# A hybrid RWKV-7 / block-attention layer on one core: ScalarE's weight split moved to the head of each RWKV chunk, and two attention score tiles moved ahead of the last chunk's root and transposed output

## The reference, cut to what matters

```
h   = RMSNorm(x);  P = h @ W_in          # columns: RWKV parts | q k v of attention | gate_A | gate_B
y_A = RWKV-7 time mixing, 8 heads of 64  # per head a 64x64 state, delta rule, then GroupNorm, bonus, gate
      per head:  y = (y - mean) * rsqrt(var + eps) * ln_w + ln_b   (+ bonus, * g)
y_B = causal block attention with ALiBi, 8 heads of 64 (softmax over scores)
x   = x + (sigmoid(gate_A) * (y_A @ W_up_A) + sigmoid(gate_B) * (y_B @ W_up_B)) @ W_o
x   = x + SwiGLU(RMSNorm(x));  out = RMSNorm(x)
```

## Time and profile before

| | |
|---|---|
| median of three runs | 932.14 us (931.51 to 936.15) |
| the profiled execution | 935.92 us, of which the span from first to last instruction is 934.1 us |
| mean granted TensorE clock over the span | 0.953 of full |
| busy: TensorE matmul, weight load | 887.8 us, 701.1 us |
| busy: VectorE, ScalarE, GpSimd | 413.5, 331.4, 120.7 us |
| RWKV chunks | from about 148 to 322 us |
| attention tiles | from about 322 to 464 us |

### The profile page before, as it was taken

How to read it: one execution, slowest core, us unless ns; L and a number is a source line. 1 busy time by engine, 2 the same in 40 slices (tenths; PEclk the granted TensorE clock), 3 DMA queues, 4 the chain that set the end, 5 groups by cost and what they waited for, 6 DMA issues and landing times.

```text
span 934.1 us, 12038 instructions
## 1 busy us (share of the span) xinstructions
PE 887.8 (95%) x4561; PEld 701.1 (75%) x4561; DVE 413.5 (44%) x600; ACT 331.4 (35%) x509; POOL 120.7 (13%) x124
## 2 busy tenths in 40 slices
PE   5999998999999969999999989999999999999996
PEld 4677766868686847666788867888888888888884
DVE  5389596241414144444466246443444344322224
ACT  5667422121212143333444145344443344211222
POOL 3054921130304011101032000000000000000000
PEclk9999999696968789999999999999999999999998
DMA  6422423210113112222233513333333332232212
GB/s 188 114 70 67 135 69 90 53 48 16 34 34 102 57 45 68 69 68 57 65 105 118 170 50 95 108 90 90 90 97 105 98 104 90 94 105 94 91 68 90
DMA packets 122298, 79.45 MB, mean 85 GB/s; under 512 B 15033, under 2 KB 110322, under 8 KB 122258
## 3 DMA queue, kind: packets, MB, share of 16 engines
q1 hardware_dynamic: 122066, 78.87, 28.5%
q0 software_dynamic: 192, 0.02, 0.0%
HBM read 73.63 MB, written 5.24 MB: 84 GB/s over the span
## 4 chain that ended last, share of the span: by engine, by line
PE 84%; DVE 8%; ACT 4%; issue 2%; DMA 1%; POOL 0%; SPq 0%; ACTq 0%; DVEq 0%
PE PS L1469 24%; PE PS L1470 23%; PE PS L1471 23%; DVE w_lo L1097 2%; PE PS L1670 2%; PE PS L1688 1%; PE PS L1565 1%; PE PS L1821 1%; DVE sq L1171 1%; PE PS L1832 1%; ACT w_hi L763 1%; PE PS L1636 1%; DVE gates L1376 1%; PE PS L1710 1%; PE PS L1607 1%
## 5 line engine op out<-in xcount | busy, mean ns | idle before, releaser
L1469 PE MATMUL PS<-hT_hi,w_hi 128*128 128x512 f32 (+1 forms) x664 | 275.4, 415 | 9.5 <-DVE gates L1376 5.5
L1470 PE MATMUL PS<-hT_lo,w_hi 128*128 128x512 f32 (+1 forms) x664 | 264.5, 398 | 0.0
L1471 PE MATMUL PS<-hT_hi,w_lo 128*128 128x512 f32 (+1 forms) x664 | 263.9, 397 | 0.0
L1097 DVE TENSOR_TENSOR w_lo<-wraw,w_hi 128x1024 fp32r<-128x1024 f32 (+1 forms) x125 | 165.4, 1324 | 181.2 <-ACT w_hi L763 179.5
L763 ACT ACTIVATE w_hi<-wraw 128x1024 fp32r<-128x1024 f32 (+1 forms) x125 | 131.4, 1051 | 135.3 <-PE PS L1471 112.6
L1469 PEld LDWEIGHTS PS<-hT_hi,w_hi 128*128 128x128 f32 (+1 forms) x664 | 127.0, 191 | 46.1 <-issue 18.6
L1471 PEld LDWEIGHTS PS<-hT_hi,w_lo 128*128 128x128 f32 (+1 forms) x664 | 127.4, 192 | 28.8
L1470 PEld LDWEIGHTS PS<-hT_lo,w_hi 128*128 128x128 f32 (+1 forms) x664 | 127.6, 192 | 24.8 <-issue 1.0
L1470 PE MATMUL PS<-w_lo,act_hi 128*128 128x512 f32 x176 | 70.2, 399 | 0.0
L1469 PE MATMUL PS<-w_hi,act_hi 128*128 128x512 f32 x176 | 69.3, 394 | 0.0
L1471 PE MATMUL PS<-w_hi,act_lo 128*128 128x512 f32 x176 | 69.0, 392 | 0.0
(11 more groups left out here) (234 smaller groups left out, 1092.3 us busy)
## 6 DMA issues: line engine op xcount, KB each, us to landing
wraw<-in_w_ffn_in_dram SPq DMA_DIRECT2D x88, 256.0 KB, 3.1
wraw<-in_w_in_dram SPq DMA_DIRECT2D x82, 256.0 KB, 3.3
wraw<-in_w_ffn_out_dram SPq DMA_DIRECT2D x44, 256.0 KB, 2.9
wraw<-in_w_o_dram SPq DMA_DIRECT2D x16, 256.0 KB, 3.1
xt<-in_x_dram SPq DMA_DIRECT2D x4, 512.0 KB, 5.2
qk_scratch<-stage SPq DMA_DIRECT2D x8, 256.0 KB, 2.7
qkT<-qk_scratch SPq DMA_DIRECT2D x4, 512.0 KB, 4.8
wraw<-in_w_up_a_dram SPq DMA_DIRECT2D x8, 256.0 KB, 3.1
```

Source lines behind the costliest of these rows:

```text
L1097: dve.tensor_tensor(w_lo[:, q, 0:n], wraw[:, s, 0:n], w_hi[:, q, 0:n].bitcast(F32), ALU.subtract)\
L1469: pe.matmul(out_, a_hi, b_hi, start=start, stop=False)
L1470: pe.matmul(out_, a_hi, b_lo, start=False, stop=False)
L1471: return pe.matmul(out_, a_lo, b_hi, start=False, stop=stop)
```

## The change

It touches the order of instructions, and adds one small one. In each chunk, ScalarE's `split_hi` of unit U_QK+2c+3 goes from behind `y_affine(c-1)` to the head of the chunk, ahead of `tokens(c)`. At the seam:

- ScalarE: a one-element Exp ACTIVATE is added ahead of `split_hi(29)`; `ystd(3)` goes behind `probs(0)`; `y_affine(3)` goes behind `probs(1)` and `probs_T(0)`; `ya_hi(3)` goes from tile 0 to tile 1.
- VectorE: `split_lo(29)` goes ahead of `y_centre(3)`; `score_bias(0)` goes ahead of `y_var(3)`; then `weights(0)`, `score_bias(1)`, `y_rstd(3)`, the gate copy of tile 0, `weights(1)`, `split_lo(30)`; `ya_lo(3)` goes to tile 1.
- TensorE: `gate(0, 1)` goes ahead of `probs_T(0)`, then `y_T(3)`; `values(0)` goes behind `gate(1, 0)` and `attn_scores(2)`.

```diff
@@ -974,11 +974,11 @@
                                scale=1.0 if n % 2 else -HD ** -0.5).then_inc(fill_ready, 1)
 
             for c in range(TT):
+                split_hi(U_QK + 2 * c + LEAD, U_QK + 2 * c + LEAD)
                 tokens(c)
                 fill_out(2 * c)
                 if c:
                     y_affine(c - 1)
-                split_hi(U_QK + 2 * c + LEAD, U_QK + 2 * c + LEAD)
                 join_32(c, 0)
                 join_32(c, 1)
                 join_64(c, 0)
@@ -989,8 +989,10 @@
                 if c + 1 < TT:
                     split_hi(U_QK + 2 * c + 1 + LEAD, U_QK + 2 * c + 1 + LEAD)
                 fill_out(2 * c + 1)
-                ystd(c)
-
+                if c + 1 < TT:
+                    ystd(c)
+
+            act.activation(warm[:, 1:2], warm[:, 0:1], ACT.Exp)
             split_hi(U_GATE + LEAD - 1, U_GATE + LEAD - 1)
 
             def probs(m):
@@ -1017,13 +1019,15 @@
                 act.activation(obT_hi[:, p, :], PS[:, 1, :], ACT.Copy).then_inc(obhi_ready, 1)
 
             probs(0)
-            y_affine(TT - 1)
+            ystd(TT - 1)
             for m in range(TT * NP_):
                 if m + 1 < TT * NP_:
                     probs(m + 1)
                 probs_T(m)
+                if m == 0:
+                    y_affine(TT - 1)
                 split_hi(U_GATE + m + LEAD, U_GATE + m + LEAD)
-                if m == 0:
+                if m == 1:
                     ya_hi(TT - 1)
                 if m % TT == TT - 1:
                     ob_hi(m // TT)
@@ -1331,10 +1335,12 @@
                 if more:
                     split_lo(U_QK + 2 * c + 1 + LEAD, U_QK + 2 * c + 1 + LEAD)
                     state(c)
+                else:
+                    split_lo(U_GATE + LEAD - 1, U_GATE + LEAD - 1)
                 y_centre(c)
-                y_var(c)
-                y_rstd(c)
-            split_lo(U_GATE + LEAD - 1, U_GATE + LEAD - 1)
+                if more:
+                    y_var(c)
+                    y_rstd(c)
 
 
             dve.memset(ss[:, 0, 0:1], 0.0).then_inc(gmul_ready, 2)
@@ -1365,17 +1371,25 @@
                 dve.tensor_tensor(obT_lo[:, p, :], PS[:, 1, :], obT_hi[:, p, :].bitcast(F32), ALU.subtract)\
                    .then_inc(oblo_ready, 1)
 
+            def gate_copy(m):
+                dve.wait_ge(w_used, U_GATE + m + 1)
+                dve.tensor_copy(gates[:, KD - 1 - m // 2, m % 2, :], PS[:, 0, :]).then_inc(gates_stored, 1)
+
             score_bias(0)
+            y_var(TT - 1)
             weights(0)
-            for m in range(TT * NP_):
+            score_bias(1)
+            y_rstd(TT - 1)
+            gate_copy(0)
+            weights(1)
+            split_lo(U_GATE + LEAD, U_GATE + LEAD)
+            for m in range(1, TT * NP_):
                 if m + 1 < TT * NP_:
                     score_bias(m + 1)
-                if m + 1 < TT * NP_:
                     weights(m + 1)
-                dve.wait_ge(w_used, U_GATE + m + 1)
-                dve.tensor_copy(gates[:, KD - 1 - m // 2, m % 2, :], PS[:, 0, :]).then_inc(gates_stored, 1)
+                gate_copy(m)
                 split_lo(U_GATE + m + LEAD, U_GATE + m + LEAD)
-                if m == 0:
+                if m == 1:
                     ya_lo(TT - 1)
                 if m % TT == TT - 1:
                     ob_lo(m // TT)
@@ -1868,11 +1882,16 @@
                 gate(m, 0)
                 if m + 1 < TT * NP_:
                     attn_scores(m + 1)
-                probs_T(m)
-                gate(m, 1)
                 if m == 0:
+                    gate(0, 1)
+                    probs_T(0)
                     y_T(TT - 1)
-                values(m)
+                else:
+                    if m == 1:
+                        values(0)
+                    probs_T(m)
+                    gate(m, 1)
+                    values(m)
 
 
             pe.wait_ge(yalo_ready, TT)
```

## The result

The changed kernel takes 886.69 us, median of four runs (885.59 to 888.3), against 931.83 us for the kernel before: the ratio is 0.9554, with a 95% interval of 0.9503 to 0.9605. The forecast was 916 us with a range of 909 to 922.5. The sign was right; the gain was 45 us where 16 were forecast.

What follows compares the result with a forecast made beforehand. TensorE was taken as the bound, its matmuls filling 95% of the span, so only its waits and low-clock stretches could give time. 4.9 us from the chunks plus 11.4 from the seam, 16.3, off 932.14 gave 916 us, range 909 to 922.5.

Steps and rivals of the forecast that it cites:

- What the clock does with part 1 is the open term: Chunks: moving the split leaves the low-clock stretches unchanged, taken as 0, bounds 3.4 us saved or lost.
- the sign of this failure: Listed under what would show the prediction wrong: more than 9 us, or less than 3, from the chunks.
- the clock gains as well: Chunks: without the 1.53 us wait the clock falls later, 1.7 us for each of four chunks; 909 us, chance 0.08.
- Part 1, the waits: Chunk head: the earlier split removes TensorE's waits at `merge_32` for VectorE's negated copy, 4.9 us over four chunks.
- The 0.9 us kept for a late load: Chunk 0: at twice the median load time, `tokens(0)` is 0.9 us late; taken as 0, kept for the range.
- Part 2, the seam: Seam: TensorE's waits of 4.0, 2.9 and 1.8 us and the low clock behind them go; 11.4 us, bounds 6 and 11.7.
- the forecast cover: Seam: GpSimd scales until 328.6, TensorE wants the result at 329.4 for `y_T(3)`, so 0.8 us to spare.
- the seam keeps half its waits: Seam: root, reciprocal and scaling come late, so TensorE stands at `y_T(3)` instead; 921.5 us, chance 0.12.
- nothing: Chunks: `minus_32` is bound by something else, so the chunk part does nothing it says; 920.7 us, chance 0.03.
- nothing measurable: Chunks and seam: new waits take the place of each old one; 932 us, chance 0.03.
- The slower one: Chunks: the clock's return fails once behind `solve`, 22.1 us of work takes 22.1 us more; 938 us, chance 0.03.

Runs made afterwards that it cites:

- late_c0: The changed kernel with ScalarE's split in its old place in chunk 0 alone; five runs at 885.40, 886.87, 887.41, 888.34 and 896.77 us.

## Why the prediction was right or wrong

**The failed step** is the one that began "What the clock does with part 1 is the open term". It read: the clock falls in chunk 0 too, where the wait is only 0.3 us, "so the small tiles bring it down, not the wait, and I take no change", with bounds of 3.4 us to either side. The runs show that the wait brings it down: it fell in none of 20 chunks without a wait and in 14 of 15 with 1.5 us. Chunk 0 was one observation of a thing that varies; the same 0.3 us brought the clock down in one of five runs of `late_c0`, and when chunk 0 had no wait it never fell there. The prediction had named the sign of this failure: more than 9 us from the chunks. The term, put at nothing, was 34.2 us (39.1 less the 4.9 of the waits), ten times its bound. The low stretches held 75.1 us, of which 34.2 is 0.46 per us; not quite half, as not all of that work goes at TensorE's clock: a group of sixteen 64x64 matmuls, from its start to the next, takes 1.90 us at 0.50 and 1.07 at 1.00. The upper end of that term was readable from the low stretches of the earlier trace rows, half of all four, 37.5 us, and should have stood in the range as one case.

**The rival "the clock gains as well"** named the right cause, the wait, but the wrong effect, and so the wrong price. It supposed that the fall would come later by 1.7 us' worth in each chunk, 6.8 us in all, and had a chance of 0.08. The fall did not come at all.

**Part 1, the waits.** Right: the four are gone. In chunk 0 the split at the head waited for its load until 158.15 and was done at 159.2, ahead of the copy, as these rows of ScalarE of the changed kernel show:

```profile
158.15 1.06 ACT L763 ACTIVATE w_hi<-wraw 128x1024 fp32r<-128x1024 f32 x1 [7.46 <-DMA wraw<-in_w_in_dram]
160.21 0.60 ACT L877 ACTIVATE V_tok<-PS 128x512 f32<-128x512 f32 x1 [1.00 <-PE PS L1594]
```

The copy still waits for TensorE, by 1.00 us, where 9.50 us stood before. The 0.9 us kept for a late load were not needed. (With the load at twice 3.3 us, 152.88 + 6.6 + 1.07 is 160.55, so the bound should have been 1.0; nothing hangs on it.)

**Part 2, the seam.** 11.8 us against 11.4. ScalarE in the changed kernel, in order of time:

```profile
280.09 1.28 ACT L995 ACT_TABLE_LOAD   x1
281.38 0.20 ACT L995 ACTIVATE warm<-warm 128x1 f32<-128x1 f32 x1
281.49 1.04 ACT L763 ACTIVATE w_hi<-wraw 128x1024 fp32r<-128x1024 f32 x1
285.71 0.40 ACT L1005 ACTIVATE Pr<-sc,nmax 128x128 f32<-128x128 f32 x1 [3.17 <-DVE nmax L1356]
...
286.61 1.28 ACT L911 ACT_TABLE_LOAD   x1
287.90 0.21 ACT L911 ACTIVATE yvar<-yvar 128x8 f32<-128x8 f32 x1
288.13 1.28 ACT L1005 ACT_TABLE_LOAD   x1
289.42 0.51 ACT L1005 ACTIVATE Pr<-sc,nmax 128x256 f32<-128x256 f32 x1
```

Three table loads, as forecast. The first is in idle time, and the exponentials start 1.5 us after `gate(0, 0)` instead of 6.2. GpSimd's scaling ends at 290.0, 0.9 us before `y_T(3)` at 290.87; the forecast cover was 0.8. `gate(1, 0)` waits 0.22 us, forecast 0.1. The rival "the seam keeps half its waits" is refuted: TensorE doesn't wait at L1738 or at `values(0)`. Here the forecast and its reasons held step by step, so the match of 11.8 with 11.4 is no luck.

**The price of a table switch.** Root and exponentials start 0.01 us after their loads end (286.61 + 1.28 = 287.89, root at 287.90; 288.13 + 1.28 = 289.41, Exp at 289.42), and the last load starts 0.02 us after the root ends (287.90 + 0.21 = 288.11). The Trainium skill ("ScalarE: Activation LUTs", section on what ACT_TABLE_LOAD costs) adds a drain of about 1.38 us per switch. Its 1.28 us for the load agrees with all three rows; the drain appears behind none of them, nor ahead of the last, and the measurement decides.

**The other rivals.** The chunk part did much more than it said, so "nothing" and "nothing measurable" are out. The slower one (the clock's return fails once) rightly took one low stretch more or less as something that can happen, but its direction was wrong, and so was its price. It let 22.1 us of work take twice as long; by the 1.90 us against 1.07 of the 64x64 group, an estimate, they would take some 17 us more.

## What to carry to other kernels

When the clock falls near a short wait again and again, price the wait at itself plus a little under half of the low stretch behind it, here 1.5 us plus 9.3 for a stretch of 20.5; and look for the wait that sits among small matmuls, where in these runs the clock stayed down longest. A fall with hardly any wait ahead of it is one observation, not the proof that waits don't matter: count falls over several chunks and runs first. If the times of one kernel spread by more than those of its variants, compare their mean clocks before explaining the difference.

## What the runs showed of the hardware that was not expected

- A wait of TensorE of 1.5 us among small matmuls brought the clock from 2.4 to 1.2 GHz in 14 of 15 chunks, one of 0.3 to 0.8 us in 5 of 11; in 20 chunks without a wait it never fell. Without a wait the same groups of 32x32 and 64x64 matmuls ran at full clock throughout.
- Once down, it stayed for 17.1 or 20.5 us in the chunks, with TensorE busy all the time, and for 3.4 or 6.8 us among 128x512 matmuls. With three projection slices in one block it was back after 10.2 or 13.6 us, but fell again in two chunks of four. What exactly it answers to was not settled.
- The times of one kernel go with its mean clock: the kernel before ran from 921.9 us (0.967) to 937.9 us (0.951) over the sets of runs, the changed kernel, without the waits at `merge_32`, only from 885.6 to 888.8. A number of falls that differs between executions fits that; it was seen in one trace per kernel and otherwise read from the mean clocks.
